# Starting every SBUF tile of 1024 bytes or more at a multiple of 64 bytes in a two-block transformer kernel on one core

## What is computed

```python
def swiglu(h, w_gate, w_up, w_down):
    return (jax.nn.silu(h @ w_gate) * (h @ w_up)) @ w_down

# first block, D_MODEL = 1024, D_FF = 2816, SEQ = 512
for i in range(2):
    x = x + 0.5 * swiglu(rms_norm(x, norm_w[i, 0]), ...)
    h = rms_norm(x, norm_w[i, 1])
    x = x + (mamba2_mixer(h, ...) if i == 0 else mla_mixer(h, ...))
    x = x + 0.5 * swiglu(rms_norm(x, norm_w[i, 2]), ...)
# second block
x = x + gate_m * hybrid_mixer(modulate(rms_norm_2(x, norm_mix), ...), ...)
h = modulate(rms_norm_2(x, norm_ffn), ...)
for e in range(16):                        # D_EXPERT = 256, top 2 of one group
    y = y + combine[..., e:e + 1] * ((silu(h @ w_gate[e]) * (h @ w_up[e])) @ w_down[e])
x = x + gate_f * y
return rms_norm_2(x, norm_final)
```

## Time and profile before

| | |
|---|---|
| median of 3 runs | 2858.04 us (2854.39 to 2858.29) |
| the profiled execution, its own time | 2858.58 us |
| its span, first to last instruction | 2857.3 us |
| TensorE busy | 2697.2 us, 94% of the span |
| TensorE weight loads (beside the matmuls) | 2187.7 us, 77% |
| VectorE / ScalarE / GpSimd busy | 57% / 25% / 28% |
| mean granted TensorE clock | 0.975 of 2.4 GHz |
| mean HBM traffic | 116 GB/s |

### The profile page before, as it was taken

How to read it: one execution, slowest core, us unless ns; L and a number is a source line. 1 busy time by engine, 2 the same in 40 slices (tenths; PEclk the granted TensorE clock), 3 DMA queues, 4 the chain that set the end, 5 groups by cost and what they waited for, 6 DMA issues and landing times. The chain is left out here.

```text
span 2857.3 us, 32762 instructions
## 1 busy us (share of the span) xinstructions
PE 2697.2 (94%) x12810; PEld 2187.7 (77%) x12810; DVE 1638.8 (57%) x2373; ACT 726.9 (25%) x1335; POOL 799.5 (28%) x804
## 2 busy tenths in 40 slices
PE   6999999999999999999999999999999898779994
PEld 5888877777778888888888789878888677666673
DVE  4343468888855545555455556544334567657766
ACT  2101125555521101111011245421001145432322
POOL 1111121121211111121111258711111311035875
PEclk9999999999999999999999999999999999979997
DMA  3333332222224435445344400023333453037995
GB/s 106 96 96 97 96 92 71 67 67 67 67 73 127 144 107 148 127 123 148 110 140 133 152 16 1 1 82 96 96 96 97 82 73 53 23 128 280 341 327 198
DMA packets 439323, 317.35 MB, mean 111 GB/s; under 512 B 33841, under 2 KB 403842, under 8 KB 438914
## 3 DMA queue, kind: packets, MB, share of 16 engines
q1 hardware_dynamic: 417048, 274.31, 33.1%
q10 hardware_dynamic: 15498, 32.54, 3.6%
q0 software_dynamic: 6624, 8.41, 0.9%
HBM read 314.67 MB, written 16.25 MB: 116 GB/s over the span
## 5 line engine op out<-in xcount | busy, mean ns | idle before, releaser
L225 POOL TENSOR_SCALAR w_hi<-w_lo_exact 128x1024 fp32r<-128x1024 f32 x369 | 413.2, 1120 | 1836.0 <-DMA w_lo_exact<-in_ffn_w_gate 409.0
L240 PE MATMUL bank<-h_hi,w_hi 128*128 128x512 f32 x1992 | 790.8, 397 | 24.7 <-DVE h_lo L312 10.6
L241 PE MATMUL bank<-h_lo,w_hi 128*128 128x512 f32 x1992 | 779.0, 391 | 0.0
L242 PE MATMUL bank<-h_hi,w_lo 128*128 128x512 f32 x1992 | 778.9, 391 | 0.0
L232 DVE TENSOR_TENSOR w_lo<-w_lo_exact,w_hi 128x1024 fp32r<-128x1024 f32 x369 | 455.6, 1236 | 141.0 <-POOL w_hi L225 140.0
L240 PEld LDWEIGHTS bank<-h_hi,w_hi 128*128 128x128 f32 x1992 | 375.9, 189 | 112.3 <-issue 19.9
L241 PEld LDWEIGHTS bank<-h_lo,w_hi 128*128 128x128 f32 x1992 | 376.3, 189 | 79.2 <-issue 3.4
L242 PEld LDWEIGHTS bank<-h_hi,w_lo 128*128 128x128 f32 x1992 | 376.0, 189 | 79.6
L240 PE MATMUL bank<-g_hi,w_hi 128*128 128x512 f32 x704 | 278.4, 396 | 0.0
L241 PE MATMUL bank<-g_lo,w_hi 128*128 128x512 f32 x704 | 278.4, 396 | 0.0
L242 PE MATMUL bank<-g_hi,w_lo 128*128 128x512 f32 x704 | 278.4, 396 | 0.0
(11 more groups left out here) (485 smaller groups left out, 3800.6 us busy)
## 6 DMA issues: line engine op xcount, KB each, us to landing
w_lo_exact<-in_ffn_w_gate SPq DMA_DIRECT2D x88, 512.0 KB, 3.8
w_lo_exact<-in_ffn_w_up SPq DMA_DIRECT2D x88, 512.0 KB, 3.9
w_lo_exact<-in_ssm_w_in SPq DMA_DIRECT2D x48, 512.0 KB, 3.9
mod_w<-in_w_mod ACTq DMA_DIRECT2D x48, 512.0 KB, 3.8
e_lo_exact<-in_w_gate SPq DMA_DIRECT2D x46, 512.0 KB, 4.9
e_lo_exact<-in_w_up SPq DMA_DIRECT2D x46, 512.0 KB, 6.2
e_lo_exact<-in_w_down SPq DMA_DIRECT2D x46, 512.0 KB, 5.5
w_lo_exact<-in_ffn_w_down SPq DMA_DIRECT2D x32, 512.0 KB, 3.7
```

What stands on the lines that cost most here:

```text
L225: ge.tensor_scalar(k.w_hi[:, u % SLOTS, :], k.raw[:, u % SLOTS, :], 1.0, 0.0, ALU.mult, ALU.add).then_inc(*k.up("w hi", u))
L240: te.matmul(k.bank[bank][:, :], hi, x_hi, start=first, stop=False)
L241: te.matmul(k.bank[bank][:, :], hi, x_lo, start=False, stop=False)
L242: return te.matmul(k.bank[bank][:, :], lo, x_hi, start=False, stop=stop)
```

## The change

One statement in the allocator: before a tile of 1024 bytes or more is placed, the base is rounded up to a multiple of 64.

```diff
     def sb(self, name, shape, dt=F32):
         size = 4
         for n in shape[1:]:
             size *= n
+        if size >= 1024:
+            self.base = (self.base + 63) // 64 * 64
         self.n_names += 1
         t = self.nc.alloc_sbuf_tensor_at(f"{name}_{self.n_names}", list(shape), dt, offset=self.base)
         self.base += (size + 31) // 32 * 32
```

## The result

The changed kernel takes **2838.65 us** (median of 5 runs, 2833.35 to 2841.77), the kernel before beside it 2856.91 us (5 runs, 2852.79 to 2858.29). The ratio is 0.9939 with an interval of 0.9926 to 0.9952: 17.4 us less, between 13.7 and 21.1. The spans of the two profiled executions are 2857.3 and 2837.4 us, 19.9 apart, against a forecast of 20.6. All lines of the changed kernel stand two further on (L240 is now L242, L2579 is L2581).

What follows compares the result with a forecast made beforehand. The prediction took TensorE's matmul rate as the bound, with loads waiting for it; savings of 14.1 + 2.2 + 1.3 + 3.0 = 20.6 us took 2858.6 to 2838.0 us, range 2831.5 to 2845.

Steps and rivals of the forecast that it cites:

- I take the difference as the price of the start: Matmuls of 512 columns: a moving tile starting off a multiple of 64 costs 6.7 ns more, 233.3 against 226.6.
- Term 1: Feed-forward down phases: 2112 matmuls at 6.7 ns less each, 14.1 us saved, all on the path.
- Term 2: Output projection of ssm: 325 of 384 matmuls gain, 2.2 us; about 60 slotted into the last scan count nothing.
- Term 3: Output projection of mla: 192 matmuls at 6.7 ns less each, 1.3 us saved.
- Term 4: Expert blocks: 576 matmuls, 3.8 us at most, counted as 3.0 because the DMA engines are near their limit.
- Terms 5 to 8: Float32 matmuls, narrow matmuls, work on VectorE, ScalarE and GpSimd, and DMA into shifted tiles: 0 each.
- The start isn't the cause: Rival, chance 0.05: the matmul distance goes with the tile's place in SBUF, so the time stays at 2858.

Runs made afterwards that it cites:

- experiment 2: The kernel before with only h_hi and h_lo moved up by 32 bytes, other large tiles keeping their starts modulo 64: 2889.69 us, ratio 1.0107.
- experiment 3: The changed kernel with the weight ring moved to 32 beyond a multiple of 64: 2892.88 us, 54 us more than the changed kernel.
- experiment 4: The kernel before with its whole space moved up by 32 bytes, all distances between tiles kept: 2851.29 us, ratio 0.9988 to the kernel before.
- experiment 6: Two variants of the changed kernel: stage tiles 128 bytes further, 2853.46 us; rounding to 128 modulo 256 instead of to 64, 2840.83 us.
- moe-only: The kernel before with only the start of the stage moe rounded up to a multiple of 64: 2853.65 us, ratio 0.9988.
- feed-forward-only: The kernel before with only the start of the four feed-forward stages' tiles (g) rounded up to a multiple of 64: 2841.0 us, ratio 0.9948.
- the paced one: The changed kernel with a wait added in moe, holding GpSimd's rounding of expert units behind VectorE's remainders: 2851.63 us, ratio 0.998.
- the first with pairs: The changed kernel with g_hi and g_lo moved by a fixed pair of offsets per feed-forward half, (0, 64) to (32, 32): 2844.56 us, one run.

## Why the prediction came out right

Time, range and sign held; the mechanism held in its size but not in its reason.

- **The step that failed** is "I take the difference as the price of the start". The rows compared tiles that were aligned with tiles that weren't, and in before every aligned tile among them also agreed with the weight ring modulo 256. Experiments 2, 3, 4 and 6 part the two: mixer's `y` at an unchanged multiple of 64 at 233.3 ns, `h` on a multiple of 64 at 235.5, `h` 32 beyond at 226.6, and the change's own rule with no gain. In the kernel before, `g`, `y` of ssm, `o` and the experts leave 96 modulo 256, the ring and the experts' stationary `xt` and `ht` 128; the change makes it 128 for all.
- What saved the number was a remark: that the shifted tiles agree with `h_hi` modulo 1024, so a coarser boundary would be met too. They do, and `h` agrees with the ring. That the ring agrees with both was luck: nothing in the forecast looked at it. With 128 bytes more ahead of the stages (experiment 6) the same forecast would have missed by some 15 us, and nothing in it would have warned.
- *Term 1, down phases:* 14.1 forecast, 14.1 measured, eight times 1.76. SP's waits rightly said that nothing else was late.
- *Term 2, ssm:* 1.9 of 2.2, and 0.7 lost ahead of it in the scan. 72 of the 384 matmuls are slotted into the scan, not about 60, so 312 remain, worth 2.1.
- *Term 3, mla:* the `o` stretch lost 2.9, but also 1.6 in the moe-only and the feed-forward-only kernel, where `o` still runs at 233.3. The difference, 1.3, is the term; 1.6 lay in this execution of before. Over mla as a whole the attention took it back.
- *Term 4, experts:* 3.0 forecast, 0.1 in the trace. Two things were off. The price: 4.4 ns a matmul instead of 6.7, 2.4 us in all; the kernel of moe alone shows the same 2.4, and why it is less than 6.7 is not shown. And the waits, which took 2.2 us back. The forecast looked for them at the transfers, but the stall that was followed came by way of GpSimd and VectorE, at a DMA share of 0.91. The whole stretch scatters by more than the gain: 235.9 to 243.3 us in the six unpaced kernels whose expert tiles agree, 237.0 to 241.3 in the four with the tiles 32 off, one execution each. Part of that is the stretch at the lower clock, which some of these executions have and others don't. Moe alone measured as a ratio that includes 1. Whether a gain exists in the median **stays open**.
- *Terms 5 to 8, at nothing:* no row speaks against them. The stretches with waits gained and lost 1 to 3 us each. Moe's beginning got 2.5 us shorter in the changed kernel, but 2.3 longer where only `g` moved, and also 2.2 and 2.5 longer in two kernels that place moe's tiles as the changed one does (the paced one and the first with pairs). So it is scatter, not the change.
- *The rivals:* "The start isn't the cause" was aimed at place, which experiment 2 refutes; the rival that was missing is the other operand. The rule of the Trainium skill ("TensorE: Matmul & The Clock Gate", section "Wait — 56ns, not 53.3ns?"), 215.7 ns at 512 columns with no term for addresses, agrees with none of the means of whole down phases here: 226.67 at best, 238.0 at worst.

## What to carry to other kernels

Where TensorE streams without a gap, read the distance of starts for each pair of moving and stationary tiles; if the same shape shows two rates, compare the residues of *both* addresses before changing one. Place the moving tiles, all of them alike, at the stationary ring's residue modulo 256 (for 512 columns of this type it was worth 3% of a matmul), and write that down as the rule, since alignment to 64 gives it only by luck. After a tile is moved, work out where the tiles behind it went: in experiments 2 and 3 they moved too. And when two groups of rows differ in one property, look for a second one in which they differ too, and move each operand by itself.

## What the runs showed of the hardware

- The distance of matmuls in this type, 512 columns, granted clock 1.00, depends on the two operands' starts relative to each other: 226.67 ns when equal modulo 256, 229.0 at 64 bytes, 231.7 at 16, 233.3 at 32, 48, 96 and 192, 232.4 or 233.3 at 128 depending on the tile, 238.0 at 4. It also depends on whether successive moving tiles agree: 232.0 with offsets 0 and 64 in turn, where either alone gave 226.67 and 229.0. At 2.4 GHz the first is 544 cycles, the most common other one 560. In the Trainium skill, "SBUF — State Buffer", section "Operand start alignment" speaks of where an operand may start; these runs add that within what is allowed it costs up to 5%. Why 256, and what exactly a moving tile with other neighbours pays, is open. Other column counts and types were not tried.
- The records of the weight loads last 188 to 189 ns on average in the changed kernel and in those of experiments 2 and 3, for `h` and `g` alike; the price shows only in the matmuls.
- VectorE's remainder of 128x1024 took 1.22 us in the median and 4.06 us beside back-to-back roundings on GpSimd. The kernel paced to avoid that cut the longest to 2.09 us and was 13 us slower.
